# Second attention layer: stick-breaking heads between the forgetting projections, and half of the output product between forgetting units

## The chip, the cores and the metric

One core of one Trainium2 chip. The metric is the device time of the whole kernel in microseconds, the median of the runs shown.

## What is computed

A first transformer block (mLSTM and grouped-query attention, then a convolutional feed-forward) is followed by a second block of two layers. The change lies in the attention mixer of the second block. It works on 256 tokens of width 1024, in float32, with 8 forgetting heads and 8 stick-breaking heads of width 64:

```python
xn = rms_norm_2(h, norm_g)
proj = xn @ w_in                       # q, k, v of 16 heads, and 8 forget logits
q, k, v = heads(...), heads(...), heads(...)
log_f = log_sigmoid(f_logit)
q_fox, k_fox, q_sb, k_sb = rms_norm_2 of each half of the heads, over the 64 of a head
# forgetting: softmax(q k' / 8 + cum_f[query] - cum_f[key], causal) @ v
# stick-breaking: z = q k' / 8; w = exp(log_sigmoid(z) + sum over later keys of log_sigmoid(-z)), key < query
#                 out = w @ v
o = concatenate([o_fox, o_sb], axis=1)
h = h + o @ w_out
```

A feed-forward layer, a short convolution mixer and another feed-forward layer follow.

## The kernel before

**The weight stream.** All weights come from memory as blocks of 128 x 1024 floats through a ring of six buffers. ScalarE (ACT) rounds a block to its high part (`whi`, L1055, `split_hi`), GpSimd (POOL) subtracts to get the low part (`wlo`, L296, `rest`; `wait_rest` waits for it), and TensorE (PE) makes each product as three matmuls, high by high, high by low and low by high (`mm3`, L440 to L442). A ring slot is free again when PE has counted the block in `blk_done`. ACT issues the splits in program order between its other work (`splits_upto`), so a split can be late because of what stands ahead of it. SP's DMA queue loads the raw blocks by itself.

**The attention mixer**, stage by stage:

1. Values: 8 blocks (`product_n`, PSUM banks 0 to 3). VectorE (DVE) copies them to `v2` (L1891).
2. Projections j = 0 to 15 (`product_t`, 24 matmuls each, banks 4 and 5 in turn): four blocks of stick-breaking queries, four of their keys, four of forgetting queries, four of their keys. A block holds two heads. For each, ACT squares it (L1348), DVE copies it to `q2` (L1895), and PE sums the squares of each head (`head_sums`, L864). After a group of four, `row_rsqrt` on ACT (L1337, L1340) and `row_rstd` on DVE (`newton`, L1462 to L1466) make the scales, `spread_rstd` on PE (L876, a matmul with 8 rows of contraction) spreads a scale row over the partitions, and `finish_qk` on DVE (L1886) multiplies. Projection j waits until DVE has copied block j-2. Before it copies block 6 DVE also makes the cumulated forget sums and constant rows, 19 instructions (L1902 to L1922): ten of them (the fills of L1911 and L1915 to L1921) are constants.
3. Stick-breaking heads h = 0 to 7, one turn of a loop each: `sb_scores(h)` (L913, L914, banks 2 and 3), `spread_rstd(8+h)`, `sb_later(h-1)` (L923 to L926, banks 4 and 5), `sb_values(h-2)` (L933 to L935, banks 6 and 7). ACT takes Abs, Exp and Ln of the scores (L1372 to L1376) and later an Exp (L1380); DVE has six operations of 384 columns a head (L1936 to L1954), two of them multiplications with both inputs in SBUF (L1943, L1954), and a `finish_qk`.
4. Forgetting units u = 0 to 15 (head u//2, query half u%2): `fox_scores(u)` (L962 to L966), `fox_transposes(u-1)` (L976), `fox_values(u-2)` (L985); DVE takes the maximum (L1965), ACT the Exp (L1387), DVE copies the transposes (L1973).
5. Eight transposes of the output (L1007, banks 4 and 5 in turn), each split by ACT (L1392) and DVE (L1985).
6. Output product: 8 blocks into banks 0 to 3 (`product_k`, each block adds to all eight tiles), the last two as a pair (`product_k_pair`). Then the norm and the feed-forward layer.

Each engine works in the order that is written; an instruction that waits holds all behind it on its engine. Line numbers are those of kernel.py of before, as in the rows.

Of the kernel before, what the change touches and what calls it, by code (L numbers as in the profile page):

```python
# [12 lines left out]
P = 128  # L13
D = 1024
KC = D // P
T = 256
# [98 lines left out]
def build(nc, xc_d, ccol_d, params_d, const_d, const1_d, const2_d, wgate_d, wf_d, stream_d, out_d):  # L115
# [3 lines left out]
    with ctx:  # L119
# [303 lines left out]
        def fin_bank(i):  # L423

            return (6 if i < 8 else 0) + i % 2
# [12 lines left out]
        def _(pe):  # L438
# [420 lines left out]
            def head_sums(i):  # L859

                g, b = i // 4, i % 4
                pe.wait_ge(S["qk_sq"], 10 + i + 1)
                pe.wait_ge(S["evac_v"], v_before + 4)
                pe.matmul(PS[0:8, g, 0:T], K0[:, C_SELQ + 16 * b:C_SELQ + 16 * b + 8], sqr2[i % 2],  # L864
                          start=b == 0, stop=b == 3).then_inc(S["st_done"], 1)

            def spread_rstd(i):

                g, b = i // 4, i % 4
                pe.wait_ge(S["rq_done"], 2 + g + 1 if i < 8 else 6)  # L870
                if i >= 2:
                    pe.wait_ge(S["qk_fin"], 10 + i - 1)
                else:
                    pe.wait_ge(S["f_add"], 1)
                    pe.wait_ge(S["spread_ready"], 2)
                pe.matmul(PS[:, fin_bank(i), 0:T], spread[0:8, P * b:P * b + P],  # L876
                          rr2[2 + g][0:8, :], start=True, stop=True).then_inc(S["fin_bc"], 1)
# [7 lines left out]
            for j in range(16):  # L885
                if j >= 2:
                    pe.wait_ge(S["evac_v"], v_before + 4 + j - 1)
                wait_rest(pe, S_ATT2 + KC + j)
                product_t(S_ATT2 + KC + j, PS[:, 4 + j % 2, 0:T], 0, T)
                if j == 1:  # L890
                    pe.wait_ge(S["wg_lo"], 2)
                    for k in range(KC):
                        mm = mm3(PS[0:8, 7, 0:T], wfh[:, k, :], wfl[:, k, :], Hh[:, k, 0:T], Hl[:, k, 0:T],
                                 k == 0, k == KC - 1)
                    mm.then_inc(S["gates2_ps"], 1)
                if j >= 1:
                    head_sums(j - 1)
                if j >= 8:
                    spread_rstd(j - 8)
            head_sums(15)  # L900
# [5 lines left out]
            def sb_scores(h):  # L906
                rows, b = half_of(h)
                if h < 2:
                    pe.wait_ge(S["qk_fin"], 18)
                    pe.wait_ge(S["rq_done"], 6)  # L910
                else:
                    pe.wait_ge(S["sb_sp"], 2 * h - 2)
                pe.matmul(PS[:, 2 + h % 2, 0:T], q2[rows, 4 + b, 0:P], q2[rows, b, :], start=True, stop=True)  # L913
                pe.matmul(PS[:, 2 + h % 2, T:T + P], q2[rows, 4 + b, P:T], q2[rows, b, P:T],  # L914
                          start=True, stop=True).then_inc(S["z_done"], 1)

            def sb_later(h):

                pe.wait_ge(S["sb_spm"], h + 1)
                if h >= 2:  # L920
                    pe.wait_ge(S["sb_arg"], h - 1)
                bank = 4 + h % 2
# [6 lines left out]
            def sb_values(h):  # L929
                pe.wait_ge(S["sb_wm"], h + 1)  # L930
                v = slice(512 + HD * h, 512 + HD * h + HD)
# [6 lines left out]
            pe.wait_ge(s_kx2, 16)  # L938
            pe.wait_ge(S["evac_v"], v_before + 20)
            for h in range(10):  # L940
                if h < 8:
                    sb_scores(h)
                    spread_rstd(8 + h)
                if 1 <= h < 9:
                    sb_later(h - 1)
                if h >= 2:
                    sb_values(h - 2)


            def fox_scores(u):  # L950
                h, qt = u // 2, u % 2
                n = P * (qt + 1)
                rows, b = half_of(h)
                if u < 2:
                    pe.wait_ge(S["sb_sp"], 16)
                    pe.wait_ge(S["cf_ready"], 3)
                    pe.wait_ge(S["qk_fin"], 26)
# [8 lines left out]
                pe.matmul(PS[:, 2 + u % 2, 0:n], q2[rows, 8 + b, P * qt:P * qt + P], q2[rows, 12 + b, 0:n],  # L966
                          start=False, stop=True, skip_group_check=True).then_inc(S["fs_done"], 1)

            def fox_transposes(u):
# [3 lines left out]
                else:  # L973
                    pe.wait_ge(S["sb_arg"], 8)
# [14 lines left out]
            for u in range(18):  # L989
                if u < 16:  # L990
                    fox_scores(u)
                if 1 <= u < 17:
                    fox_transposes(u - 1)
                if u >= 2:
                    fox_values(u - 2)

            for i in (4, 5, 6, 7, 0, 1, 2, 3):
                n = (i - 4) % 8
                pe.wait_ge(S["sb_out"], 2)
                if i < 4:  # L1000
                    pe.wait_ge(S["fox_out"], 2)
                if n >= 2:
                    pe.wait_ge(S["t2_lo"], n - 1)
                else:
                    pe.wait_ge(S["fox_exp"], 16)
                for tt in range(2):
                    mm = pe.transpose(PS[:, 4 + n % 2, P * tt:P * tt + P], o2[:, tt, P * i:P * i + P], ident)  # L1007
                mm.then_inc(S["t2_ps"], 1)
            for i in range(KC - 2):
                wait_rest(pe, S_OUT2 + i)  # L1010
                pe.wait_ge(S["t2_lo"], 8)
                product_k(S_OUT2 + i, Hh[:, i, 0:T], Hl[:, i, 0:T], i == 0, False)
            for i in (KC - 2, KC - 1):
                wait_rest(pe, S_OUT2 + i)
# [1177 lines left out]
```

## Time and profile before

| | us |
|---|---|
| runs | 1451.11, 1442.70, 1443.71 (median 1443.71) |
| profiled execution | 1446.88 |
| its span, first to last instruction | 1445.0 |
| PE busy | 1339.4 (93%) |
| DVE busy | 820.2 (57%) |
| ACT busy | 635.8 (44%) |
| POOL busy | 699.6 (48%) |
| values projected | about 715 to 740 |
| projections | 740 to 813.6 |
| stick-breaking | 817 to 863.9 |
| forgetting | 864 to 889.3 |
| output transposes | 889.3 to 896.9 |
| output product | 896.9 to 922.2 |

The last six lines are positions in the span. A matmul's start is measured and its end is modelled, so a time from start to start is the safer figure. "Clock" is the share of the full 2.4 GHz that was granted to TensorE: 1.00 is 2.4 GHz and 0.50 is 1.2 GHz.

### The profile page before, as it was taken

The numbers are of one execution on the slowest core, as the hardware profiler recorded it, in microseconds if no ns is written. First come the engines' busy times: TensorE is split into PE (matmuls) and PEld (weight loads), VectorE is DVE, ScalarE is ACT, GpSimd is POOL, SyncE is SP. The second block draws the span as 40 slices with busy tenths as digits, with TensorE's granted clock in tenths as the row PEclk, the third lists the DMA queues.
The fourth block names the chain that finished last, engine by engine and source line by source line (L and its number), as shares of the span: only waits on it lengthen the run. The fifth ranks groups of instructions, "written<-read, shape, count | busy, mean of one in ns | idle before, by whom it ended". The sixth has DMA issues, their size and how long they took to land. (4 is left out here: it accounts for less than half of the span.)

```text
span 1445.0 us, 25596 instructions
## 1 busy us (share of the span) xinstructions
PE 1339.4 (93%) x9656; PEld 1204.7 (83%) x9656; DVE 820.2 (57%) x1363; ACT 635.8 (44%) x1084; POOL 699.6 (48%) x296
## 2 busy tenths in 40 slices
PE   5879989979999989999898998899999998899998
PEld 0657869957679989999786676899999898799998
DVE  3530025368552467666615554277777788577776
ACT  2422233225453455555533333455455443655543
POOL 1443452224126735557584300456557577455564
PEclk9999999979999999999999758999999999899999
DMA  9676441112114625556463200345456455354552
GB/s 376 227 263 226 161 132 59 59 30 92 56 53 138 186 92 174 177 188 217 124 188 104 88 0 1 88 161 188 174 179 203 129 162 164 105 182 174 175 174 103
DMA packets 57742, 208.50 MB, mean 144 GB/s; under 512 B 6576, under 2 KB 7600, under 8 KB 57408
## 3 DMA queue, kind: packets, MB, share of 16 engines
q1 hardware_dynamic: 57168, 205.55, 42.6%
q0 software_dynamic: 496, 1.87, 0.3%
q8 instruction: 53, 0.87, 0.2%
q14 instruction: 25, 0.20, 0.0%
HBM read 206.35 MB, written 1.05 MB: 144 GB/s over the span
## 5 line engine op out<-in xcount | busy, mean ns | idle before, releaser
L296 POOL TENSOR_TENSOR wlo<-raw,whi 128x1024 fp32r<-128x1024 f32 x284 | 693.9, 2461 | 708.1 <-ACT whi L1055 708.1
L440 PE MATMUL ps<-Hh,whi 128*128 128x256 f32 (+2 forms) x1976 | 582.2, 295 | 39.4 <-DVE Hl L2016 7.6
L441 PE MATMUL ps<-Hl,whi 128*128 128x256 f32 (+2 forms) x1976 | 571.5, 289 | 0.0
L442 PE MATMUL ps<-Hh,wlo 128*128 128x256 f32 (+2 forms) x1976 | 571.1, 289 | 0.0
L440 PEld LDWEIGHTS ps<-Hh,whi 128*128 128x128 f32 (+1 forms) x1976 | 385.0, 195 | 62.9 <-issue 24.5
L1055 ACT ACTIVATE whi<-raw 128x1024 fp32r<-128x1024 f32 x338 | 351.9, 1049 | 157.3 <-DMA raw<-in_stream 69.5
L441 PEld LDWEIGHTS ps<-Hl,whi 128*128 128x128 f32 (+1 forms) x1976 | 385.8, 195 | 2.7
L442 PEld LDWEIGHTS ps<-Hh,wlo 128*128 128x128 f32 (+1 forms) x1976 | 384.9, 195 | 2.7
L1839 DVE SCALAR_TENSOR_TENSOR arena<-ps,sm,arena 128x255 f32<-128x255 f32 (+1 forms) x264 | 127.2, 483 | 100.9 <-ACT arena L1302 92.6
L440 PE MATMUL ps<-dh,whi 128*128 128x256 f32 x592 | 170.3, 288 | 10.8 <-DVE wlo L1815 3.5
L441 PE MATMUL ps<-dl,whi 128*128 128x256 f32 x592 | 169.4, 286 | 0.0
L442 PE MATMUL ps<-dh,wlo 128*128 128x256 f32 x592 | 169.3, 286 | 0.0
L1302 ACT ACTIVATE arena<-ps,sm 128x256 f32<-128x256 f32 x132 | 66.6, 504 | 156.8 <-DVE ps L1829 130.5
L440 PEld LDWEIGHTS ps<-dh,whi 128*128 128x128 f32 x592 | 115.6, 195 | 12.2 <-issue 6.6
L441 PEld LDWEIGHTS ps<-dl,whi 128*128 128x128 f32 x592 | 115.8, 196 | 0.0
L442 PEld LDWEIGHTS ps<-dh,wlo 128*128 128x128 f32 x592 | 115.6, 195 | 0.0
L1850 DVE TENSOR_TENSOR dl<-arena,dh 128x256 fp32r<-128x256 f32 x60 | 77.0, 1284 | 30.9 <-ACT dh L1312 30.9
L1815 DVE TENSOR_TENSOR wlo<-raw,whi 128x1024 fp32r<-128x1024 f32 x54 | 67.9, 1257 | 0.0
L1810 DVE COPY sm<-params 128x8 f32 (+1 forms) x66 | 59.4, 904 | 8.1 <-DVE arena L1839 7.6
L1312 ACT ACTIVATE dh<-arena 128x256 fp32r<-128x256 f32 x60 | 25.1, 418 | 86.5 <-DVE arena L1847 85.8
L470 PE MATMUL ps<-whi,Hh 128*128 128x512 f32 (+1 forms) x128 | 48.2, 376 | 4.0 <-DVE Hl L1518 4.0
L472 PE MATMUL ps<-whi,Hl 128*128 128x512 f32 (+1 forms) x128 | 47.4, 370 | 0.0
(291 smaller groups left out, 1429.9 us busy)
## 6 DMA issues: line engine op xcount, KB each, us to landing
raw<-in_stream SPq DMA_DIRECT2D x386, 512.0 KB, 4.2
X<-in_xc SPq DMA_DIRECT2D x2, 1024.0 KB, 10.5
out_y<-X SPq DMA_DIRECT2D x8, 128.0 KB, 1.9
kx<-in_const POOLq DMA_DIRECT2D x1, 512.0 KB, 6.9
arena<-in_wgate POOLq DMA_DIRECT2D x1, 400.0 KB, 8.9
params<-in_params POOLq DMA_DIRECT2D x1, 372.0 KB, 6.9
k<-in_const POOLq DMA_DIRECT2D x1, 256.0 KB, 4.9
kx<-in_const POOLq DMA_DIRECT2D x1, 256.0 KB, 4.1
```

Of the source, the lines that this page charges most:

```text
L296: pool.tensor_tensor(wlo[:, slot, :], raw[:, rslot, :], whi[:, slot, :].bitcast(f32), ALU.subtract).then_inc(rest_done[0], 1)
L440: pe.matmul(out, lh, rh, start=start, stop=False, skip_group_check=True)
L441: pe.matmul(out, lh, rl, start=False, stop=False, skip_group_check=True)
L442: return pe.matmul(out, ll, rh, start=False, stop=stop, skip_group_check=True)
L470: pe.matmul(out, Hh[:, k, tok], wh_, start=k == 0 and first, stop=False, skip_group_check=True)
L472: pe.matmul(out, Hl[:, k, tok], wh_, start=False, stop=False, skip_group_check=True)
L1055: act.activation(whi[:, s % RING, :], raw[:, r % RING, :], ACT.Copy).then_inc(hi_done, 1)
L1302: act.activation(tc, PS[:, 4 + 2 * slot + j, 0:T], ACT.Identity, bias=bias, scale=cwb[:, slot, 3 * j:3 * j + 1]).then_inc(S["centre"], 1)
L1810: dve.tensor_copy(cwb[:, i % 2, :], src).then_inc(S["cw_copy"], 1)
L1815: dve.tensor_tensor(wlo[:, s % RING, :], raw[:, RAW_OF_W[s] % RING, :], whi[:, s % RING, :].bitcast(f32), ALU.subtract).then_inc(rest_done ...
L1839: dve.scalar_tensor_tensor(tc[:, lo:hi], u[:, src:src + hi - lo], cwb[:, slot, 3 * j + 1 + n:3 * j + 2 + n], tc[:, lo:hi], ALU.mult, ALU.a ...
L1850: dve.tensor_tensor(lo, h, hi.bitcast(f32), ALU.subtract).then_inc(S["down_lo"], 1)
```

## The change

- The weight stream brings query block and key block of the same two heads next to each other (sb q0, k0, q1, k1, ... then forgetting q0, k0, ...), and the blocks of the output product in the order 4, 5, 6, 7, 0, 1, 2, 3.
- The scales are spread from projection 6 on into the free upper half of the banks of the projections (`fin_out`); the row sums of group g go to bank g%2; `spread2` is a table of its own in `kx`.
- The stick-breaking heads run between projections 8 to 15, which are the forgetting ones. `sb_later` uses the scores' own bank (2 or 3), so its DVE reader frees it for the scores two heads on.
- The constant rows move on DVE ahead of the copies of the values; only the forget sums stay in the loop, ahead of `finish_qk(0)`.
- The forgetting units start while the last stick-breaking heads end. Four spreads go into units 2 to 5, four output transposes (of the stick-breaking half of the output, into banks 0 and 1) into units 8 to 11, and the first half (four of eight tiles) of the product of the first four output blocks into units 13 to 16. The second halves follow with the other four transposes between them, then blocks 4 and 5, and 6 and 7 as a pair.

The host's layout follows. The diff, cut to PE's order, DVE's order and what they call (ACT's order follows the same indices):

```diff
+        spread2 = KX[:, C2_N:2 * C2_N]
+
+        def fin_out(i):
+
+            return PS[:, 4 + i % 2, T:2 * T] if i < 8 else PS[:, 0 if i < 12 else i % 2, 0:T]
+
+        def fin_before(i):
+
+            return i - 1 if i < 13 else i - 2
...
+                if g >= 2 and b == 0:
+                    pe.wait_ge(S["rq_done"], 1 + g)
+                pe.matmul(PS[0:8, g % 2, 0:T], K0[:, C_SELQ + 16 * b:C_SELQ + 16 * b + 8], sqr2[i % 2],
...
+                pe.wait_ge(S["rq_done"], 3 + g)
+                pe.wait_ge(S["spread_ready"], 2)
+                if i > 8:
+                    pe.wait_ge(S["qk_fin"], 10 + fin_before(i) + 1)
+                pe.matmul(fin_out(i), spread2[0:8, P * b:P * b + P], rr2[2 + g][0:8, :],
+                          start=True, stop=True).then_inc(S["fin_bc"], 1)
...
-            for j in range(16):
+            def project(j):
+
                 if j >= 2:
                     pe.wait_ge(S["evac_v"], v_before + 4 + j - 1)
+                if j >= 8:
+                    pe.wait_ge(S["qk_fin"], 10 + min(j - 7, 8))
...
-                if h < 2:
-                    pe.wait_ge(S["qk_fin"], 18)
-                    pe.wait_ge(S["rq_done"], 6)
-                else:
-                    pe.wait_ge(S["sb_sp"], 2 * h - 2)
-                pe.matmul(PS[:, 2 + h % 2, 0:T], q2[rows, 4 + b, 0:P], q2[rows, b, :], start=True, stop=True)
-                pe.matmul(PS[:, 2 + h % 2, T:T + P], q2[rows, 4 + b, P:T], q2[rows, b, P:T],
-                          start=True, stop=True).then_inc(S["z_done"], 1)
-
-            def sb_later(h):
-
-                pe.wait_ge(S["sb_spm"], h + 1)
+                pe.wait_ge(S["qk_fin"], 10 + 2 * b + 2)
                 if h >= 2:
                     pe.wait_ge(S["sb_arg"], h - 1)
-                bank = 4 + h % 2
+                pe.matmul(PS[:, 2 + h % 2, 0:T], q2[rows, 2 * b + 1, 0:P], q2[rows, 2 * b, :], start=True, stop=True)
+                pe.matmul(PS[:, 2 + h % 2, T:T + P], q2[rows, 2 * b + 1, P:T], q2[rows, 2 * b, P:T],
+                          start=True, stop=True).then_inc(S["z_done"], 1)
+
+            def sb_later(h):
+
+                pe.wait_ge(S["sb_sp"], 2 * h + 2)
+                pe.wait_ge(S["sb_spm"], h + 1)
+                bank = 2 + h % 2
                 pe.matmul(PS[:, bank, 0:T], tri, sbS[h % 2][:, 0:T], start=True, stop=False, skip_group_check=True)
                 pe.matmul(PS[:, bank, P:T], ones, sbS[h % 2][:, T:T + P], start=False, stop=True,
...
+                pe.wait_ge(S["qk_fin"], 10 + 8 + 2 * b + 2)
                 if u < 2:
-                    pe.wait_ge(S["sb_sp"], 16)
+                    pe.wait_ge(S["sb_arg"], 7 + u)
                     pe.wait_ge(S["cf_ready"], 3)
-                    pe.wait_ge(S["qk_fin"], 26)
                 else:
                     pe.wait_ge(S["fox_exp"], u - 1)
...
+            def out_transposes(n):
+
+                i = (n + 4) % 8
+                if n < 4:
+                    bank = n % 2
+                    pe.wait_ge(S["sb_out"], 2)
+                    pe.wait_ge(S["qk_fin"], 26)
+                else:
+                    bank = 4 + n % 2
+                    pe.wait_ge(S["fox_out"], 2)
+                if n % 4 >= 2:
+                    pe.wait_ge(S["t2_lo"], n - 1)
+                for tt in range(2):
+                    mm = pe.transpose(PS[:, bank, P * tt:P * tt + P], o2[:, tt, P * i:P * i + P], ident)
+                mm.then_inc(S["t2_ps"], 1)
+
+            def out_rows(n):
+
+                i = (n + 4) % 8
+                return Hh[:, i, 0:T], Hl[:, i, 0:T]
+
+            def out_half(n, half):
+
+                wait_rest(pe, S_OUT2 + n)
+                if half == 0:
+                    pe.wait_ge(S["t2_lo"], 4)
+                else:
+                    pe.wait_ge(S["fox_exp"], 16)
+                for m in range(4 * half, 4 * half + 4):
+                    mm = mm3(PS[:, m // 2, (m % 2) * T:(m % 2) * T + T], *w(S_OUT2 + n, m), *out_rows(n),
+                             n == 0 and m % 2 == 0, False)
+                if half == 1:
+                    mm.then_inc(blk_done, 1)
+
+            for j in range(16):
+                project(j)
+                if j == 1:
+                    forget_gates()
+                if 6 <= j:
+                    spread_rstd(j - 6)
+                if j >= 1:
+                    head_sums(j - 1)
+                if j >= 8:
+                    sb_scores(j - 8)
+                if j == 9:
+                    pe.wait_ge(s_kx2, 16)
+                if j >= 9:
+                    sb_later(j - 9)
+                if j >= 10:
+                    sb_values(j - 10)
+            head_sums(15)
+            spread_rstd(10)
+            fox_scores(0)
+            sb_values(6)
+            spread_rstd(11)
+            sb_later(7)
+            fox_scores(1)
+            fox_transposes(0)
+            sb_values(7)
+            for u in range(2, 18):
                 if u < 16:
                     fox_scores(u)
-                if 1 <= u < 17:
+                if u < 6:
+                    spread_rstd(10 + u)
+                if 8 <= u < 12:
+                    out_transposes(u - 8)
+                if u < 17:
                     fox_transposes(u - 1)
-                if u >= 2:
...
+                if 13 <= u < 17:
+                    out_half(u - 13, 0)
+                fox_values(u - 2)
+            for n in range(4):
+                out_half(n, 1)
+                if n == 1:
+                    out_transposes(4)
+                if n >= 1:
+                    out_transposes(4 + n)
+            for n in (4, 5):
+                wait_rest(pe, S_OUT2 + n)
+                pe.wait_ge(S["t2_lo"], n + 1)
+                product_k(S_OUT2 + n, *out_rows(n), False, False)
+            for n in (6, 7):
+                wait_rest(pe, S_OUT2 + n)
+            pe.wait_ge(S["t2_lo"], 8)
+            product_k_pair(S_OUT2 + 6, out_rows(6), S_OUT2 + 7, out_rows(7))
...
+            link(dve.tensor_scalar(selr, K0[:, 0:8], 0.0, None, ALU.mult))
+            link(dve.tensor_copy(selr[0:8, :], ident[0:8, 0:8]))
+            link(dve.tensor_copy(selr[32:40, :], ident[32:40, 32:40]))
+            link(dve.tensor_copy(identr, ident))
+            for qt in range(2):
+                link(dve.tensor_scalar(maskr[qt], K0[:, 0:T], 0.0, None, ALU.mult))
+                link(dve.tensor_copy(maskr[qt][:, P * qt:P * qt + P], maskA))
+            for rows_r in (cfk, cfq):
+                link(dve.tensor_scalar(rows_r, K0[:, 0:T], 0.0, None, ALU.mult))
...
+            for j in range(18):
+                if j in (5, 9, 13, 17):
+                    row_rstd((j - 5) // 4)
+                if j == 6:
+                    forget_sums()
+                if 7 <= j < 17:
+                    finish_qk(j - 7)
+                if j == 17:
+                    fox_maximum(0)
+                    finish_qk(10)
+                if 0 <= j - 10 < 8:
+                    sb_exponents(j - 10)
+                if 0 <= j - 9 < 8:
+                    sb_terms(j - 9)
+                if 0 <= j - 10 < 8:
+                    sb_masked(j - 10)
+                if j < 16:
+                    dve.wait_ge(S["qk_sq"], 10 + j + 1)
+                    dve.tensor_copy(q2[:, j, :], PS[:, 4 + j % 2, 0:T]).then_inc(S["evac_v"], 1)
...
+
+
+            for u in range(1, 17):
+                if u < 16:
+                    fox_maximum(u)
+                if u == 1:
+                    finish_qk(11)
+                if 2 <= u < 6:
+                    finish_qk(10 + u)
+                fox_turned(u - 1)
+                if u == 1:
+                    dve.wait_ge(S["sbv_done"], 8)
                     for qt in range(2):
-                        link(dve.tensor_scalar(maskr[qt], K0[:, 0:T], 0.0, None, ALU.mult))
-                        link(dve.tensor_copy(maskr[qt][:, P * qt:P * qt + P], maskA))
-                    dve.memset(fr[0], 1.0).then_inc(S["cf_ready"], 1)
...
+                        dve.tensor_copy(o2[:, qt, 512:1024], PS[:, 6 + qt, :]).then_inc(S["sb_out"], 1)
+                if 9 <= u < 13:
+                    out_lo(u - 9)
...
-    for c in (512, 1536, 0, 1024):
-        wlist += [*blocks_t(w2, ar_(c, c + 512))]
-    wlist += [*blocks_k(inp["attn_w_out_2"][0])]
+    for q_at, k_at in ((512, 1536), (0, 1024)):
+        for q_, k_ in zip(blocks_t(w2, ar_(q_at, q_at + 512)), blocks_t(w2, ar_(k_at, k_at + 512))):
+            wlist += [q_, k_]
+    wo = blocks_k(inp["attn_w_out_2"][0])
```

## Rows read from the trace of the kernel before

**Rows 1.** Page, part 2: granted clock of TensorE, 40 slices of 36.1 us.

```profile
PEclk9999999979999999999999758999999999899999
```

**Rows 2.** Busy time by stretch: start:end, length, PE PEld DVE ACT POOL busy (count), clock, DMA share, GB/s.

```profile
770.50:777.00 6.50, 0.00 (x0) 0.00 (x0) 5.97 (x16) 0.80 (x1) 2.34 (x1) 0.86 0.49 163
777.00:782.40 5.40, 5.34 (x25) 5.21 (x26) 1.98 (x6) 0.00 (x0) 0.00 (x0) 0.53 0.01 3
...
813.50:817.00 3.50, 0.09 (x2) 0.04 (x1) 2.55 (x5) 0.88 (x2) 2.17 (x1) 0.89 0.40 114
817.00:859.60 42.60, 42.60 (x126) 32.03 (x127) 21.62 (x45) 15.44 (x31) 0.00 (x0) 0.50 0.03 12
...
864.00:889.30 25.30, 24.41 (x152) 18.39 (x151) 12.07 (x35) 8.19 (x32) 0.00 (x0) 1.00 0.00 1
889.30:897.00 7.70, 4.05 (x20) 2.41 (x18) 4.50 (x10) 2.96 (x8) 0.00 (x0) 0.63 0.01 2
897.00:922.20 25.20, 25.20 (x192) 25.00 (x192) 0.76 (x2) 6.62 (x7) 14.40 (x6) 0.91 0.40 114
```

**Rows 3.** Timeline of DVE after projection 5: start, us, what.

```profile
767.92 2.41 DVE L1911 TENSOR_SCALAR Hh<-k 128x256 fp32r<-128x256 f32 x1
...
771.12 0.29 DVE L1911 TENSOR_SCALAR Hh<-k 128x256 fp32r<-128x256 f32 x1
...
774.34 0.17 DVE L1915 TENSOR_SCALAR Hh<-k 128x8 fp32r<-128x8 f32 x1
...
776.46 0.27 DVE L1922 MEMSET arena<- 128x256 f32 x1
```

**Rows 4.** Timeline of ACT, squares of projections 13 and 14.

```profile
803.50 0.38 ACT L1348 ACTIVATE arena<-ps 128x256 f32<-128x256 f32 x1 [2.88 <-PE ps L442]
...
807.71 0.38 ACT L1348 ACTIVATE arena<-ps 128x256 f32<-128x256 f32 x1 [2.09 <-PE ps L442]
```

**Rows 5.** Timeline of PE, one stick-breaking turn, then the last two heads.

```profile
830.30 1.22 PE L913 MATMUL ps<-arena 64*128 64x256 f32 x2
...
831.88 1.22 PE L876 MATMUL ps<-arena 8*128 8x256 f32 x2
833.02 1.22 PE L923 MATMUL ps<-arena,kx 128*128 128x256 f32 x2
834.03 0.64 PE L924 MATMUL ps<-arena,k 128*128 128x128 f32 x2
...
834.89 0.53 PE L933 MATMUL ps<-arena 128*128 128x64 f32 x2
...
836.20 1.22 PE L913 MATMUL ps<-arena 64*128 64x256 f32 x2
...
860.60 0.39 PE L924 MATMUL ps<-arena,k 128*128 128x128 f32 x2
...
861.05 0.33 PE L933 MATMUL ps<-arena 128*128 128x64 f32 x2
...
863.00 0.43 PE L933 MATMUL ps<-arena 128*128 128x64 f32 x2 [1.17 <-DVE arena L1954]
```

**Rows 6.** Timelines of ACT and DVE: the last row scales, then one head.

```profile
813.67 0.47 ACT L1337 ACTIVATE arena<-ps,sm 8x256 f32<-8x256 f32 x1 [0.41 <-PE ps L864]
...
831.98 0.49 ACT L1372 ACTIVATE arena<-ps 128x384 f32<-128x384 f32 x1 [1.37 <-PE ps L914]
...
816.43 0.41 DVE L1466 SCALAR_TENSOR_TENSOR arena<-arena 8x256 f32<-8x256 f32 x1
...
834.55 0.55 DVE L1943 TENSOR_TENSOR arena<-arena,kx 128x384 f32<-128x384 f32 x1
```

**Rows 7.** PE in the first layer's attention, and the stretch behind it (columns of rows 2).

```profile
343.75 1.13 PE L727 MATMUL ps<-arena 64*128 64x512 f32 x4 [1.67 <-DVE arena L1678]
...
345.00:348.50 3.50, 3.50 (x12) 1.93 (x12) 3.50 (x6) 1.69 (x3) 1.86 (x1) 0.52 0.09 28
```

**Rows 8.** Busy time while the values are projected, columns as in rows 2.

```profile
722.00:748.00 26.00, 26.00 (x150) 22.31 (x149) 3.33 (x6) 10.67 (x12) 25.68 (x12) 1.00 0.67 202
```

More of the change, by code:

```diff
@@ L883, in _, with forget_gates @@
                           norm=2)
-            for j in range(16):
+            def project(j):
                 if j >= 2:
                     pe.wait_ge(S["evac_v"], v_before + 4 + j - 1)
+                if j >= 8:
+                    pe.wait_ge(S["qk_fin"], 10 + min(j - 7, 8))
                 wait_rest(pe, S_ATT2 + KC + j)
                 product_t(S_ATT2 + KC + j, PS[:, 4 + j % 2, 0:T], 0, T)
[L890 to L900, printed above, removed]
+            def forget_gates():
+                pe.wait_ge(S["wg_lo"], 2)
+                for k in range(KC):
+                    mm = mm3(PS[0:8, 7, 0:T], wfh[:, k, :], wfl[:, k, :], Hh[:, k, 0:T], Hl[:, k, 0:T],
+                             k == 0, k == KC - 1)
+                mm.then_inc(S["gates2_ps"], 1)
             def half_of(h):
@@ L936, in sb_values @@
                           stop=True).then_inc(S["sbv_done"], 1)
[L938 to L947, printed above, removed]
             def fox_scores(u):
@@ L1009, in _ @@
[L1009 to L1014, printed above, removed]
-            product_k_pair(S_OUT2 + KC - 2, (Hh[:, KC - 2, 0:T], Hl[:, KC - 2, 0:T]),
-                           S_OUT2 + KC - 1, (Hh[:, KC - 1, 0:T], Hl[:, KC - 1, 0:T]))
+                if u < 6:
+                    spread_rstd(10 + u)
@@ L1388, in _ @@
                                accum_out=foxsum[:, col:col + 1]).then_inc(S["fox_exp"], 1)
-            for n in range(8):
-                i = (n + 4) % 8
-                act.wait_ge(S["t2_ps"], n + 1)
-                act.activation(Hh[:, i, 0:T], PS[:, 4 + n % 2, 0:T], ACT.Copy).then_inc(S["t2_hi"], 1)
+                if 9 <= u < 13:
+                    out_hi(u - 9)
+            for n in range(4, 8):
+                out_hi(n)
             for i in range(KC):
@@ new lines, in sb_terms @@
+            def sb_terms(h):
+                z, L, sp, lb = PS[:, 2 + h % 2, 0:384], sbL[h % 2], sbS[h % 2], sbB[h % 2]
+                dve.wait_ge(S["sb_l"], 3 * h + 3)
+                if h >= 2:
+                    dve.wait_ge(S["r_done"], h - 1)
+                dve.scalar_tensor_tensor(sp, z, 0.0, L, ALU.max, ALU.add).then_inc(S["sb_sp"], 1)
+                if h >= 2:
+                    dve.wait_ge(S["sb_arg"], h - 1)
+                dve.scalar_tensor_tensor(lb, z, 0.0, L, ALU.min, ALU.subtract).then_inc(S["sb_sp"], 1)
+                if h == 0:
+                    dve.wait_ge(s_kx2, 16)
+                dve.wait_ge(S["sb_sp"], 2 * h + 1)
+                dve.tensor_tensor(sp, sp, strict, ALU.mult).then_inc(S["sb_spm"], 1)
@@ L1981, in _ @@
                    .then_inc(S["fox_out"], 1)
-            for n in range(8):
-                i = (n + 4) % 8
-                dve.wait_ge(S["t2_hi"], n + 1)
-                dve.tensor_tensor(Hl[:, i, 0:T], PS[:, 4 + n % 2, 0:T], Hh[:, i, 0:T].bitcast(f32), ALU.subtract)\
-                   .then_inc(S["t2_lo"], 1)
+            for n in range(4, 8):
+                out_lo(n)
             add_and_norm_late(3, S_FFN2 - 1, lambda k: pr("fnorm0", k, k + 1))
```

232 lines of the change are left out of this document (96 added, 136 removed).

## The prediction

> **What bounds the kernel now.** I read the page's clock line first. TensorE has its full clock nearly everywhere and loses it in the slices from 795 to 903 us [rows 1], which is where the second attention mixer is. Then I cut that stretch by stage. PE does nothing from 770.5 to 777.0 and from 813.5 to 817.0; between 817.0 and 859.6 it is busy without a pause (42.6 of 42.6 us) at a clock of 0.50; the forgetting units run at 1.00 and PE is busy 24.4 of 25.3 us; from 889.3 to 897.0 it is busy 4.05 of 7.7 us; the output product takes 25.2 us, its first part at half clock (0.91 over the stretch) [rows 2]. DVE and ACT are busy at most 21.6 of 42.6 us in the stick-breaking stage [rows 2]. So this region is bound by PE at half speed and by PE waiting. The change gives PE nothing less to compute; what it can win is clock and waits. I add up positions in the span of the profiled execution (1445.0, its own time 1446.9, 3.2 above the median of 1443.7) and take the difference from the median.
>
> **Part 1, the forget sums.** PE stops at 770.4 and its next product starts at 777.0, at half clock: 24 matmuls in 5.34 us [rows 2]. DVE is in the forget block until 776.7 [rows 3]. Ten of its nineteen instructions move ahead of the value copies: the two fills, 2.41 and 0.29 us, and the eight from 774.34 to 776.46, 2.1 us [rows 3]. DVE then ends 4.8 us sooner, at 771.9, copies block 6 (0.4) and finishes block 0 (0.5), which product 8 now awaits: 772.8. PE itself, with two spreads of 0.57, would be ready at 771.5. So product 8 starts at 773.0. The 2.41 us fill is the 0.29 us fill that met a GpSimd subtraction; the next instruction in line may meet it instead, so the bounds are 771.5 and 775. The ten moved instructions meet GpSimd, which is busy 25.7 of 26 us while the values are projected [rows 8]. At 2.4 us each they need some 22 us of a stretch in which DVE works 3.3 us; the copies of the values would end near 745 and project 2 starts at 749. I price them at zero; without this cover they would cost at most the 4.8 us that they gave.
>
> The Trainium skill (GPSIMD Engine Reference, its table's row on SBUF interfaces) says that GpSimd shares its interfaces with VectorE and contends with instructions that have two SBUF inputs or run in a two-port mode. The fills of 2.41 and 0.29 us agree. By this rule the two masking multiplications of each head (both inputs in SBUF) are exposed too, now that GpSimd works beside them; that is rival 3.
>
> **Part 2, stick-breaking between projections.** One turn at half clock is 5.90 us from L913 to L913: scores 1.58, spread 1.14, later 1.87, values 1.31 [rows 5]. At full clock the step from L924 to L933 is 0.45 us where it was 0.86 [rows 5], a factor of 1.9; I halve: 0.79, 0.57, 0.93, 0.65. A late projection of before with its head sum and its spread takes 4.21 us [rows 4]. Products 8 to 15 then cost 4.21+0.79 = 5.0, 5.9 with `sb_later`, and six times 6.58 = 39.5: PE leaves the loop at 773.0+50.4 = 823.4, with the last product ended at 819.9. That this is at full clock is my choice: each turn has 24 dense matmuls, and the half-speed product at 777 was followed by full clock [rows 2]. DVE and ACT stay hidden: a head needs 3.1 us from the scores (ACT starts at 831.98) to the masked terms (DVE ends at 835.10) [rows 6], and PE has about 6 us of other work between `sb_scores(h)` and `sb_later(h)`. DVE's load in a turn is some 3.4 us (seven operations of 0.42 to 0.55), ACT's 3.6 us with the weight split.
>
> **Part 3, the seam.** After product 15 PE has 4.0 us of queued work and then depends on two chains. (a) Head sum 15 ends at +4.0; then ACT Ln and Exp, DVE's four newton steps (from the Ln's start at 813.67 to 816.84 it took 3.2 us [rows 6]), the maximum of unit 0 and `finish_qk(10)`: `spread_rstd(11)` can start at +8.15, while PE has run out at +6.3. It stands ahead of `sb_later(7)`. (b) `sb_later(7)`, DVE's exponents, `fox_scores(1)`, then ACT's Exp for unit 0: two further waits, 0.7 and 0.35 us. Unit 2 starts at +12.3, that is 832.2 at full clock. There are 2.9 us of waiting in 5.1 us, and all other work there is narrow matmuls.
>
> What does the clock do? Before, PE waited 1.67 us at 342.1, did narrow float32 matmuls, and the clock was at half from 345.2 [rows 7]. It waited 1.17 us at 861.8 [rows 5] and stayed at full [rows 2]. The seam's 1.85 us with 0.7 behind it is nearer to the first, so I take it that the clock falls. Then it comes back late: stick-breaking, busy throughout, stayed at half for 42.6 us [rows 2], and forgetting units are the same kind of work. Only the half products from unit 13 on are dense.
>
> The Trainium skill (TensorE: Matmul & The Clock Gate, Why this matters for your kernels) warns only of idle gaps over about 3 us. By this rule the seam is harmless, which is rival 1. The 1.67 us of rows 7 speaks against it.
>
> **Part 4, the forgetting units.** Units 2 to 17 took 23.3 us (866.0 to 889.3). Added: four spreads 2.4, four output transposes 2.4 (eight take 4.05 us of PE in rows 2, some of it at half clock), four half products of 12 dense matmuls 5.8, and 1.0 for `fox_values(0)`, which awaits the two copies of the stick-breaking output. At full clock: 34.9, until 867.1.
>
> **Part 5, the output product.** Four second halves 5.8, four transposes 2.2, blocks 4 and 5 5.8, GpSimd's low part of block 7 late by 0.6 (ACT splits blocks 6 and 7 only after the last transpose), the pair 5.8: 20.2, so the end is 887.3 instead of 922.2. All at full clock the change wins 34.9 us.
>
> **Part 6, half clock from the seam on.** Seam +1.6; units 2 to 12 cost 1.52 us each at full clock and, by a factor between 1.75 (dense matmuls) and 1.95 (rows 5), 1.85 at half: 11 x 1.3 = 14.3; spreads 2.2; transposes 2.0; units 13 and 14 2.5; the first half product 1.1; the wait of `fox_values(0)` gone, -1.0. Sum 22.7, bounds 18 and 27. The win shrinks to 12.2 us: **1443.7 - 12.2 = 1431.5 us**, its own range 1426 to 1437.
>
> **The rivals.**
>
> 1. *The clock holds through the seam.* For it: 1.17 us did no harm [rows 5]. Against it: 1.67 us did [rows 7]. 1443.7 - 34.9 = 1408.8.
> 2. *The clock falls, but comes back early in the forgetting units*, say in unit 7. For it: these units hold 256-column matmuls that stick-breaking lacks. Against it: 42.6 us without return [rows 2]. Cost 1.6+6.5+2.2-1.0 = 9.3, so 1443.7 - 25.6 = 1418.
> 3. *DVE becomes the bound of products 9 to 15.* Both masking multiplications of a head wait out a GpSimd subtraction: 3.4+4.8 = 8.2 us a turn against PE's 6.58, 1.6 x 7 = 11 us. With part 6 nothing is left: 1443. Against it: GpSimd makes one subtraction of 2.4 us per turn, so it can hardly be met twice.
> 4. *Slower.* The half clock sets in at product 8 (PE waits 1.5 us ahead of it) and the interleaved turns never get it back: six turns of 12.3 instead of 6.58 us, and 9.7 more for the first two, 44 us. With part 6: 1443.7 - 12.2 + 44 = 1475. For it: stick-breaking matmuls never raised the clock [rows 2]. Against it: the dense product inside each turn. It decides from about two turns at half clock on (12.2/5.7 = 2.1).
>
> **How the numbers follow.** Forecast 0.46, rival 1 0.17, rival 2 0.21, rival 3 0.10, rival 4 0.06. One per cent, about what a measurement of this kernel can tell from no change, is 14.4 us: below 1429.3. Rivals 1 and 2 are faster by that (0.38), and about three tenths of the forecast's share (0.14): 0.52. Slower is rival 4, 0.06. The rest is 0.42. The range is 1408 to 1441: below it is half of rival 1, above it rival 4 and half of rival 3.
>
> **What would show it.** Right: no PE idle near 770 over 2 us; products 10 to 15 with starts 6.6 us apart at clock 1.00; a PE wait of 1.5 to 2.2 us ahead of L876's spread 11, released by DVE; then clock 0.50 and forgetting units at 2.8 us each until the half products. Wrong: clock 1.00 behind the seam (rival 1), projections further apart than 7 us, or L440 waiting for DVE copies in them (rivals 3, 4).

## The result and the profile after

The changed kernel takes 1430.17 us, the median of 8 runs (1427.3 to 1437.3); the kernel before, on the same chip, takes 1444.21 us (8 runs, 1438.6 to 1451.1). The ratio is 0.9899, 95% interval 0.9872 to 0.9926: about 14 us or 1% faster, where 1431.5 was predicted. Executions more than 1.5% above the fastest of their kernel are left out of ratios and intervals, here and below, but not out of medians. The profiled execution took 1427.29 us (span 1425.4).

The positions of the two traces can't be subtracted directly. Project 2 starts at 739.62 where it started at 748.83: 9.2 us that arose upstream of the mixer (among others the half clock of [rows 7] is missing in this execution). From the start of project 2 to the end of the output product the mixer took 173.4 us before (748.83 to 922.2) and takes 160.2 us now (739.62 to 899.87). That is the win of the change in the profiled pair: 13.1 us, beside 12.2 predicted.

The granted clock on the page of after, 40 slices of 35.6 us, answers to [rows 1]. The loss is in the same place and a little shorter:

```profile
PEclk9999999979999999999999957999999999899999
```

By stretch, the columns of [rows 2]: product 8, the interleaved turns, the forgetting units, then the last units and the second halves.

```profile
765.19:771.72 6.53, 6.53 (x33) 5.46 (x33) 1.04 (x3) 1.22 (x2) 1.87 (x1) 0.74 0.35 123
...
778.00:815.00 37.00, 37.00 (x251) 30.98 (x250) 22.04 (x45) 19.02 (x36) 13.51 (x6) 1.00 0.29 86
...
824.00:875.00 51.00, 50.31 (x177) 38.19 (x177) 16.05 (x41) 9.12 (x35) 0.00 (x0) 0.50 0.00 1
875.00:888.00 13.00, 13.00 (x107) 12.54 (x106) 3.67 (x9) 2.00 (x7) 0.00 (x0) 0.99 0.00 1
```

Stick-breaking had 42.6 us at 0.50 and the forgetting units had 1.00 [rows 2]. Now the interleaved stretch has 1.00 with PE busy 37.0 of 37 us, and the half clock has moved to the forgetting units: PE is busy 50.3 of 51 us at 0.50. PE's waits from 725 to 912 us (engine, line waited for: total, count, longest):

```profile
PE ps L446 <- DVE Hl L1857: 6.0, 1, 6.0
PE ps L882 <- DVE arena L1951: 1.5, 1, 1.5
PE ps L446 <- DVE arena L2054: 1.5, 1, 1.5
PE ps L882 <- DVE arena L1531: 1.1, 1, 1.1
PE ps L955 <- issue: 0.7, 1, 0.7
PE ps L926 <- DVE arena L1993: 0.7, 1, 0.7
PE ps L446 <- POOL wlo L296: 0.6, 1, 0.6
```

The first is the norm behind the product. The second is the seam's wait, the third the one ahead of product 8 (6.5 us before, [rows 2]), the last the low part of block 7. The fourth and the sixth had no counterpart in the prediction. Line numbers are those of the changed kernel: L882 `spread_rstd`, L926 `sb_later`, L955 `fox_scores`, L996 output transposes, L1951 `finish_qk`.

### The profile page after: what moved, and what is told of

It is laid out like the page before. It is cut to its first block and busy times, and to the rows that moved or that the text cites. A ratio compares the mean times of both kernels' runs of the same rounds, so it can differ in the third digit from the quotient of the medians.

```text
span 1425.4 us, 25619 instructions
## 1 busy us (share of the span) xinstructions
PE 1328.5 (93%) x9656; PEld 1200.8 (84%) x9656; DVE 834.6 (59%) x1363; ACT 634.6 (45%) x1084; POOL 699.1 (49%) x296
## 5 line engine op out<-in xcount | busy, mean ns | idle before, releaser
L1875 DVE COPY sm<-params 128x8 f32 (+1 forms) x66 | 64.6, 983 | 8.1 <-DVE arena L1904 7.6
L479 PE MATMUL ps<-wlo,Hh 128*128 128x512 f32 (+1 forms) x128 | 47.1, 368 | 0.0
```

Of the source, the lines that this page charges most:

```text
L479: mm = pe.matmul(out, Hh[:, k, tok], wl_, start=False, stop=k == KC - 1, skip_group_check=True)
L1875: dve.tensor_copy(cwb[:, i % 2, :], src).then_inc(S["cw_copy"], 1)
```

## The experiments

Each ran beside the kernel before, and not all on the same chip, so where two experiments are compared the ratios count and not the medians alone. In the diffs `dense` is a helper that issues matmuls of 128 x 128 by 128 x 256, of the kind that `mm3` issues, with a result that nobody reads. They only add work: in a run of products at full clock the starts lie 0.12 us apart, so I count 0.11 to 0.12 us for each.

**Dense work at the seam.**

```diff
             sb_values(6)
+            pe.wait_ge(S["evac_v"], v_before + 20)
+            dense(PS[:, 5, 0:T], 14)
             spread_rstd(11)
             sb_later(7)
+            dense(PS[:, 5, 0:T], 6)
             fox_scores(1)
```

> The changed kernel with 14 dense matmuls (128x128 by 256 columns, result unused) ahead of spread 11 and 6 ahead of fox_scores(1), where PE waited 1.54 us and 0.69 us. Theory (the waits of the seam let the clock fall, and the forgetting units then run at half clock until the half products): the clock stays at 1.00 through the units, the stretch from the seam to the half products shrinks by some 20 us and the kernel by 18 to 22, to about 1410. Rival (the forgetting units lose the clock by themselves, whatever stands ahead of them): at most 1 us either way, and clock 0.50 in the units.

1420.2 us (1410.0, 1430.4, 1432.2, 1409.7), ratio 0.9813 (0.972 to 0.9907). The median says little, since the time has two values, and the ratio counts one of the two slower runs only. The values are those of rival 1 (1408.8) and of the forecast. The mean granted clock of the four runs was 0.970, 0.957, 0.955 and 0.970. The trace is of the first run:

```profile
824.00:875.00 51.00, 50.75 (x349) 42.14 (x349) 24.15 (x62) 15.61 (x50) 2.28 (x2) 1.00 0.04 11
```

So with the seam's waits covered the clock held in two executions and, by time and mean clock, was lost in two; neither my theory nor its rival had that. Held in two of four here and in none of eight of the change, it suggests that the waits are a cause, and not the only one. The two values also price the half clock within one program on one chip: 21.4 us (1431.3 less 1409.8, each the mean of two).

**The two seam steps exchanged.** `finish_qk(10)`, which spread 11 awaits, then runs beside `sb_later(7)`.

```diff
             sb_values(6)
-            spread_rstd(11)
             sb_later(7)
+            spread_rstd(11)
             fox_scores(1)
```

> The changed kernel with sb_later(7) moved ahead of spread_rstd(11). The wait ahead of spread 11 should shrink from 1.5 to about 0.7 us, and the wait for the exponents of head 7 nearly go. Theory that waiting time decides the clock: it stays full, 18 to 22 us faster, as with filler. Rival (narrow float32 matmuls with even short waits are too little to hold it): half clock as before and at most 1 us faster.

1419.4 us (1420.2, 1423.6, 1418.7, 1409.4), ratio 0.9794 (0.9738 to 0.985), below the change's 0.9872 to 0.9926. That is about half of the gain that I expected, with a wait that went to 0.6 us as foreseen. Waits of PE from 812 to 890, then two stretches:

```profile
PE ps L882 <- DVE arena L1951: 0.6, 1, 0.6
```
```profile
828.00:839.00 11.00, 10.45 (x55) 7.04 (x55) 7.19 (x19) 2.92 (x11) 0.00 (x0) 1.00 0.01 1
839.00:867.00 28.00, 28.00 (x106) 22.48 (x106) 7.98 (x23) 5.75 (x22) 0.00 (x0) 0.51 0.00 1
```

One wait of 0.6 us at 828 stands where 1.54 and 0.69 stood, and the clock went through the seam at full. It fell at 839, in units 2 to 6, where PE had not waited for 10 us. These units hold only `fox_scores` (three matmuls of 128 x 128 by 128 x 256, then others of only 64 rows of contraction), spreads of 8 rows, 128-column transposes and 64-column `fox_values`; I call such work thin. Here a PE that was busy with thin work lost the clock.

**Dense work in the units, with the exchange.**

```diff
                 fox_values(u - 2)
+                if 2 <= u < 13:
+                    dense(PS[:, 4 + u % 2, 0:T], 4)
```

> The changed kernel with sb_later(7) ahead of spread 11, and 4 dense matmuls (result unused) behind the values of each of the units 2 to 12, 11 x 4 x 0.12 = 5.3 us of added work. Theory now (the units' own matmuls, narrow and of float32, are too thin to hold the clock in every execution, wait or no wait): every execution keeps 1.00 through the units, all runs lie within a few us of 1409 + 5 = 1414, and the spread between runs shrinks. Rival (the clock is lost in the seam alone): some runs near 1414 and some with the clock lost, above 1430.

1413.1 us (1412.5, 1413.0, 1419.0, 1413.2), ratio 0.9817 (0.9772 to 0.9861). The kernel does 44 matmuls (4.8 us) more than the one before it. Its median is 6 us lower and its ratio a little higher, and the intervals overlap, so that it is faster isn't shown. It is no slower in spite of the added work, its four runs have mean clocks of 0.968 to 0.971 (0.957 to 0.969 there), and its trace has full clock throughout:

```profile
828.00:875.00 47.00, 46.39 (x326) 39.14 (x325) 20.27 (x54) 10.74 (x40) 0.00 (x0) 1.00 0.01 2
```

**Dense work in the units, with the seam as it was.** The same edit, without the exchange of the two steps, so that the two kernels differ in the place of one step and issue the same instructions.

> The changed kernel with its own order at the seam (waits of 1.5 and 0.7 us), and four extra dense matmuls behind the values of units 2 to 12 (44 matmuls whose result nobody reads, 4.8 us at full clock). It tells the seam's waits from the thin units. Theory A (the waits at the seam make the clock fall, thin units only keep it down): the profile shows 0.50 from about 824, the dense matmuls bring it back within a few units, 1418 to 1425. Theory B (the thin work makes it fall, the waits only add to it): with dense work from unit 2 on it does not fall in most runs, 1413 to 1416, 1.0 above the kernel with the two steps exchanged. If the dense matmuls did nothing, 1430 plus 7, so 1437.

1430.6 us (6 runs, 1425.5 to 1436.6), ratio 0.9895 (0.9845 to 0.9946). Waits from 812 to 890, then three stretches:

```profile
PE ps L882 <- DVE arena L1959: 1.5, 1, 1.5
PE ps L955 <- issue: 0.7, 1, 0.7
```
```profile
819.00:832.00 13.00, 11.46 (x70) 8.74 (x70) 8.02 (x18) 5.27 (x10) 3.00 (x2) 0.99 0.25 81
832.00:866.00 34.00, 33.31 (x117) 25.15 (x117) 9.92 (x25) 4.96 (x19) 0.00 (x0) 0.50 0.00 0
866.00:890.00 24.00, 24.00 (x182) 21.42 (x182) 8.65 (x24) 5.16 (x20) 0.00 (x0) 1.00 0.01 1
```

In the profile the wait of 1.5 us ended at 830.6 and the clock was at half from 832 to 866, in spite of four dense matmuls in each unit from 840.5 on. So theory A holds for the fall, and my time for it (1418 to 1425) was too low. The fill matmuls run at half clock too: 17 us less of half clock than the 51 of after give back about 8 us, and the 44 matmuls cost about as much. The seam's waits are 2.2 us here (1.53 and 0.69) and 0.6 us with the exchange: 1.6 us more of waiting cost 17 us by the medians and 11 by the ratios, whose intervals overlap a little; no run of one kernel lies among those of the other.

**The first half products behind the last unit.**

```diff
-                if 13 <= u < 17:
-                    out_half(u - 13, 0)
                 fox_values(u - 2)
             for n in range(4):
+                out_half(n, 0)
+            for n in range(4):
                 out_half(n, 1)
```

> The changed kernel with the four first half products behind the last unit instead of in units 13 to 16. Theory (they bring the clock back): half clock lasts past 875 us, to the dense product behind the units, so units 14 to 17 and the first half product run at half: 5 to 8 us slower, about 1436. Rival (they hide nothing and only move): within 1 us of 1430.

1438.0 us (10 runs, 1435.6 to 1442.1), ratio 0.9954 (0.9933 to 0.9976), some 8 us slower than the change. The half clock lasts until the last unit is done:

```profile
835.00:889.00 54.00, 53.11 (x183) 39.76 (x183) 18.64 (x47) 9.70 (x37) 0.00 (x0) 0.50 0.00 1
```

The half products are the same work in either place. Between the units they bring the clock back sooner, as expected.

**Transposes and half products two units sooner** (with the exchange; ACT's and DVE's splits move along).

```diff
-                if 8 <= u < 12:
-                    out_transposes(u - 8)
+                if 6 <= u < 10:
+                    out_transposes(u - 6)
...
-                if 13 <= u < 17:
-                    out_half(u - 13, 0)
+                if 11 <= u < 15:
+                    out_half(u - 11, 0)
```

> The changed kernel with sb_later(7) ahead of spread 11, and the first four output transposes and half products two units sooner (units 6 to 9 and 11 to 14). Theory: the clock comes back two units sooner in the runs that lose it, some 3 us off the slower runs and nothing off the others: about 1416 where the reordering alone had 1419. Rival (transposes beside earlier units make new waits): no gain.

1416.1 us (1412.7, 1416.1, 1423.9, 1416.1), ratio 0.9842 (0.9786 to 0.9897). By ratios it can't be told from the exchange alone; its profile has 20 us of half clock (837 to 857).

**The same with two, and with four, dense matmuls in units 2 to 10.**

> As the one before, with two extra dense matmuls a unit instead of four (18, about 1.9 us). If half as many hold the clock as well: 1409 to 1412 in every run. If they do not: runs between 1412 and 1424, and a stretch of 0.50 in the units of the profile.

> The changed kernel with the last two seam steps exchanged, the transposes and half products two units sooner, and four extra dense matmuls behind the values of units 2 to 10 (36 matmuls whose result nobody reads, about 3.9 us at full clock). Theory: the narrow work between the projections and the half products is what loses the clock; with dense work in each unit it holds in every execution: 1411 to 1414, runs within 2 us of each other, clock 1.00 from 825 to 870. Rival: the clock is a matter of luck whatever is in the units: runs spread over 1412 to 1424 as without the extra matmuls.

With two: 1414.9 us (1415.0, 1414.8, 1409.1, 1422.9), ratio 0.9787 (0.9723 to 0.9852). With four: 1412.1 us (1407.9, 1410.5, 1413.7, 1416.2), ratio 0.9767 (0.9722 to 0.9812). The latter is the lowest median measured here. Its four runs have mean clocks of 0.969 to 0.970, so the spread of 8 us that is left doesn't look like the clock of this stretch, and my "within 2 us of each other" was wrong. With two, three runs have 0.969 to 0.973 and one has 0.961 and 1422.9: by its mean clock, two matmuls a unit don't always do. No trace shows that run. The stretch with four:

```profile
820.00:870.00 50.00, 48.58 (x331) 40.20 (x330) 23.06 (x60) 11.94 (x43) 0.00 (x0) 1.00 0.04 11
```

**The constants alone, and the constants back.** The first is the kernel before with only the ten constant instructions moved ahead of the value copies. The second is the change without that move.

> The kernel before with only the ten constant instructions of DVE moved ahead of the value copies. Forecast of part 1 of the prediction: PE's wait ahead of product 8 shrinks from 6.6 to about 2 us and the product after it keeps the clock in part: 5 to 7 us faster. Rival (another subtraction of GpSimd is met instead): the wait shrinks by only 2.4 us.

> The changed kernel with the ten constant instructions back in the loop, ahead of the forget sums. Theory: they lengthen the wait ahead of product 8 by about the 4.8 us that they gave before (with them moved alone, the wait of the kernel before fell from 6.6 to 1.8 us and the time by about 5 us), so about 1435. Rival A: product 8 now has another wait that ends last (the low part of a weight block), the constants are hidden: 1430. Rival B: the longer wait also takes the clock in products 8 and 9 and the turns behind them do not get it back at once: 1440 or more. If B, the profile shows 0.50 in products 10 and 11.

Moved alone: ratio 0.9946 (0.9924 to 0.9968), about 8 us by this ratio and 6 by the medians of the executions that it counts (1438.1 beside 1444.5). Put back: 1436.9 us (1432.2 to 1440.1), ratio 0.9928 (0.9905 to 0.9952), where the change has 0.9899: 4 us, though the intervals overlap. The waits ahead of product 8, from the kernel before and from the two:

```profile
PE ps L440 <- DVE arena L1895: 6.6, 1, 6.6
```
```profile
PE ps L440 <- DVE arena L1905: 1.8, 1, 1.8
```
```profile
PE ps L446 <- DVE arena L2052: 6.3, 1, 6.3
```

From 6.6 to 1.8 us there and from 6.3 to 1.5 here: 4.8 us both times, as in Part 1. Rival A is out, and so is B: the half clock around that wait ends at 783 us, in product 8.

The kernel with the constants moved alone has two values as well: four of its twelve executions took 1456.4 to 1462.7 us, at mean clocks of 0.934 to 0.938 where the other eight have 0.952 to 0.955, and the trace is of one of the four. It has the same wait of 3.4 us ahead of stick-breaking as the kernel before, but the clock then stays at half through the forgetting units too, up to the output product:

```profile
809.00:864.00 55.00, 52.75 (x161) 40.08 (x162) 27.00 (x56) 17.49 (x36) 0.32 (x1) 0.50 0.04 10
864.00:915.00 51.00, 47.57 (x174) 36.61 (x175) 14.96 (x40) 10.24 (x36) 0.00 (x0) 0.50 0.00 1
```

The kernel before does the like: 14 of the 53 executions beside these experiments took 1461.1 to 1468.1 us at mean clocks of 0.929 to 0.936 (none of the 8 beside the change did). No trace of it in such an execution was taken.

**Dense work beside stick-breaking, in the kernel before.** In the first kernel 28 dense matmuls fill the wait at 813.5 [rows 2]; in the second there are 12 more at the end of each of the loop's ten turns.

```diff
+            pe.wait_ge(S["rq_done"], 5)
+            dense(PS[:, 2, 0:T], 28)
             pe.wait_ge(s_kx2, 16)
...
                 if h >= 2:
                     sb_values(h - 2)
+                    dense(PS[:, 4 + h % 2, 0:T], 12)
+                else:
+                    dense(PS[:, 4 + h % 2, 0:T], 12)
```

> The kernel before with 28 dense matmuls (result unused) in the wait of 3.4 us ahead of the stick-breaking heads, nothing else changed. If the stick-breaking stage was slow by the clock alone, it takes some 23 us instead of 43 and the kernel is about 20 us faster (near 1424), without any interleaving. Rival (these matmuls need dense work beside them to keep the clock, so that the interleaving is what wins): the clock falls within the stage, and the gain is under 5 us.

> The kernel before with 28 dense matmuls in the wait ahead of the stick-breaking heads and 12 in each of the ten turns of their loop (14 us of added work at full clock, result unused). Theory (stick-breaking alone is too thin to hold the clock; with dense work in each turn it holds it): the stage takes about 23 + 14 = 37 us instead of 43 in spite of that work, at clock 1.00. The forgetting units behind it have nothing dense and may lose the clock, as with the filler ahead of the heads alone: 1438 if they hold it, up to 1460 if not. Rival (the chain of ACT and DVE bounds the turns at full clock): clock 1.00 but more than 40 us, with waits for DVE.

Filling the wait alone made it slower, which neither my theory nor its rival had: 1461.8 us (1461.0 to 1462.3), ratio 1.0101 (1.0066 to 1.0136). With dense work in every turn: 1438.2 us (1435.2 to 1443.2), ratio 0.9969 (0.995 to 0.9988), in spite of 120 matmuls more in the turns (14 us) beside the 28 in the wait. Two stretches of the first, one of the second:

```profile
821.00:858.00 37.00, 37.00 (x116) 28.78 (x116) 19.29 (x41) 12.76 (x25) 0.00 (x0) 0.50 0.00 1
...
862.00:917.00 55.00, 51.57 (x189) 39.51 (x190) 15.79 (x43) 11.52 (x41) 0.00 (x0) 0.50 0.00 1
```
```profile
817.00:861.00 44.00, 43.37 (x284) 36.81 (x283) 26.14 (x55) 17.18 (x38) 0.00 (x0) 1.00 0.01 4
```

The wait at 813.5 was not what bound stick-breaking: with it filled the clock fell at 821 all the same, came back at 858, fell again at 862 and took all forgetting units with it. Before, it came back at 860.6, just ahead of these units [rows 5], and held. The four times are no new value: the kernel before takes as long in some executions, 1466.9 in one of its 14 beside this one. The fill made that outcome the usual one; what in it does so is not shown, and a wait of 0.86 us at 859 stands just ahead of the second fall. With dense matmuls in each turn the clock stays at 1.00 throughout stick-breaking, as in the change.

## Why the prediction was right

By its own steps, on the timeline of after. "Predicted" for the seam and the units is full clock plus its share of Part 6.

| stretch | predicted us | measured us |
|---|---|---|
| project 2 to product 8, time won | 4.0 | 2.6 (28.17 - 25.57) |
| product 8 until PE leaves the loop | 50.4 | 53.0 (765.19 to 818.18) |
| from there to unit 2 | 8.8 + 1.6 | 10.6 (to 828.77) |
| units 2 to 17 with the half products | 34.9 + 21.1 | 51.9 (to 880.71) |
| the rest of the output product | 20.2 | 19.2 (to 899.87) |

The last four come to 137.0 predicted and 134.7 measured; with the first, 12.2 - 1.4 + 2.3 = 13.1 us won. That the total came out within a microsecond is partly luck: 4.0 us lost in the first two rows (1.4 and 2.6) and 5.1 us less in the last two nearly cancel.

**Part 1: right, with one wait missed.** The constants met GpSimd as foreseen. DVE among the value copies, the first row that was slowed and the last:

```profile
712.46 2.38 DVE L1956 CAST Hh<-k 8x8 fp32r<-8x8 f32 x1
...
726.81 4.80 DVE L1962 TENSOR_SCALAR Hh<-k 128x256 fp32r<-128x256 f32 x2
```

They took from 712.1 to 731.6, 19.5 us where I had 22, and hid. Missed was that the row scales, which feed the first spread, can meet GpSimd as well. DVE then:

```profile
753.42 1.82 DVE L1529 SCALAR_TENSOR_TENSOR arena<-arena 8x256 f32<-8x256 f32 x1
755.28 2.50 DVE L1530 TENSOR_TENSOR arena<-arena 8x256 f32<-8x256 f32 x1
757.81 0.41 DVE L1531 SCALAR_TENSOR_TENSOR arena<-arena 8x256 f32<-8x256 f32 x1
...
760.77 2.50 DVE L1977 TENSOR_TENSOR Hh<-arena,Hh 8x256 fp32r<-8x256 f32 x1
```

L1530 and L1977, of 8 partitions, take 2.50 us where the same lines took 0.41 at 799.53 and 763.62. The first gives PE's wait of 1.1 us ahead of spread 0, and the forget sums end 2.1 us later than they could: that helps to keep product 8 at 1.5 us of waiting, the size that I had (773.0 less 771.5) without this delay. The Trainium skill (SBUF — State Buffer, SBUF: two separate sides) calls the port pair of VectorE and GpSimd an exclusive lock, held for a whole instruction, with the other side fully blocked; the trace agrees: a cast of 8 x 8 elements (2.38 us at 712.46) loses as much as the fills of 128 x 256 (4.80 for two), about one subtraction each.

**Part 2: right in its rate, 2.6 us short at its start.** PE, the start of two turns:

```profile
791.63 0.36 PE L446 MATMUL ps<-Hh,whi 128*128 128x256 f32 x1
...
798.24 0.36 PE L446 MATMUL ps<-Hh,whi 128*128 128x256 f32 x1
```

6.61 us a turn, 6.58 predicted, at clock 1.00. Product 8 took 6.53 us instead of 5.0, since the clock was at half from 766 to 769 behind the wait (0.74 in its stretch). Product 9 took 6.70 instead of 5.9, with a wait of 0.7 ahead of the first `sb_later`: DVE was late with the masked terms, behind row scales of which L1529 took 1.86 us (0.41 at 820.54). The two experiments with dense work in the kernel before bear out the reason that I gave for the full clock: with it in each turn the clock held, with it in the wait alone it fell.

**Rival 3** has no trace. DVE from 778 to 818 us, grouped by line, has both maskings at 0.55 us:

```profile
L2007 DVE TENSOR_TENSOR arena<-arena,kx 128x384 f32<-128x384 f32 x6 | 3.3, 550 | 0.0
L1993 DVE TENSOR_TENSOR arena<-arena,kx 128x384 f32<-128x384 f32 x6 | 3.3, 548 | 0.0
```

**Rival 4** had its condition and not its end: the clock fell in product 8 as it says, but was back after 3 us, by the end of that product.

**Part 3: the seam is as described, its reason incomplete.** PE after the loop:

```profile
822.70 0.67 PE L882 MATMUL ps<-arena,kx 8*128 8x256 f32 x2 [1.54 <-DVE arena L1951]
...
824.06 0.55 PE L929 MATMUL ps<-arena,kx 128*128 128x128 f32 x2
...
825.30 0.55 PE L955 MATMUL ps<-Hh 128*128 128x256 f32 x1 [0.69 <-issue]
...
828.77 0.56 PE L955 MATMUL ps<-Hh 128*128 128x256 f32 x1
```

1.54 us where I had 1.85, 0.69 where I had 0.7; the third wait (0.35) is absent. The row at 824.06 is the first at half clock. That these waits make the clock fall in this kernel is shown by the exchange, which alone takes 10.8 us off the median, and by the pair with dense units, where every run with the waits has a mean clock of 0.962 or less and every run with the exchange 0.968 or more. That the waits were needed for it is refuted: it also fell 10 us behind a wait of only 0.6 us, and, by the mean clock, in two of four runs with dense work in their place. The rule of rival 1 (the Trainium skill, TensorE: Matmul & The Clock Gate, Why this matters for your kernels: to avoid a drop, leave no idle gap of PE over some 3 us) would have given 1408.8. The measurement decides against it here: the clock fell behind gaps of 1.54 and 0.69 us.

**Parts 4 to 6: right in kind, the two terms of the output transposes too large.** PE at half clock, a unit with a transpose of the output:

```profile
849.71 0.56 PE L955 MATMUL ps<-Hh 128*128 128x256 f32 x1
...
851.36 0.69 PE L996 MATMUL ps<-k,arena 128*128 128x128 f32 x2
851.84 0.63 PE L970 MATMUL ps<-k,arena 128*128 128x128 f32 x2
...
852.55 0.56 PE L955 MATMUL ps<-Hh 128*128 128x256 f32 x1
```

Units without extra work take 2.7 us (from 844.26 to 849.71 for two), against 2.8 predicted. An output transpose takes about 0.5 us at half clock, where I had 1.1 (0.6 + 0.5): with four that is 2.4 of the 4.1 us by which the units came out shorter. The clock was back at 875, at the end of the second half product, where I had it back after the first. What half clock costs from the seam on was 22.7 in the sum; the two values of the kernel with dense work at the seam lie 21.4 us apart.

Part 5's wait of 0.6 us for GpSimd's low part is there as predicted. The sum was right because the seam's clock was, and that step had the largest chance only by a comparison of two single rows (1.67 us did harm, 1.17 did not). The reason given for rival 2 misreads the rows: stick-breaking has 256-column matmuls too (L913 and L923, [rows 5]). And "42.6 us without return" ended in thin work, at 860.6 [rows 5].

## What to carry to other kernels

Where a page shows PE busy at half clock, ask what its matmuls are, not only where it waits: thin steps ran at half clock for 20 to 55 us in the traces here, and for 105 in one, while PE was busy nearly all the time. By the mean clocks, four dense matmuls in each unit kept full clock in every run with the exchange at the seam (8 of 8) and in none with its longer waits (0 of 6). Which property of the matmuls matters, their size or their type, was not tested. Work that was moved from a thin stage into a dense one ran at full clock, and what is left behind as thin work is where the clock was lost next; putting some dense work there, even work that is thrown away, may pay. At the border of a thin stage a wait of one or two microseconds can cost many times its length (1.6 us cost 11 to 17 here), so exchange steps there first. And take more than one execution before you believe a fill or a removed wait: the same kernel came out 20 us apart.

## What the hardware showed that I had not expected

- Filling a wait made the kernel slower: with the 3.4 us ahead of stick-breaking filled, all four executions took 1461.0 to 1462.3 us, where the kernel before has 1445.0 and, in one of its 14 executions beside it, 1466.9. In the trace the clock came back at 858 and fell again at 862, instead of coming back at 860.6 and staying. When it returned in thin work looks like chance in these kernels.
- The same program has its clock in some executions and not in others: 1409.7 and 1432.2 us for one kernel, with mean clocks of 0.970 and 0.955.
- A VectorE cast of 8 x 8 elements took 2.38 us beside GpSimd (712.46), a multiplication of 8 x 256 (L1530) took 2.50 instead of 0.41.
